# Gate and up with weights stationary, down one expert behind, and requests' rows on four column groups, in a two-layer decoder step

## The chip, the cores and the metric

One core of a Trainium2 chip. The time is that of one execution on the device, in microseconds. TensorE (PE) multiplies, VectorE (DVE) and ScalarE (ACT) work on the results, GpSimd (POOL) and SyncE (SP) mostly issue transfers. The stationary operand of a matmul is loaded into the array (PEld in the profile), the moving one streams past it. An f32 matmul appears as two records, each with its own weight load.

## What is computed

One inference step of two layers on 512 prompt rows and 8 rows of single-token requests, D = 1024, all in float32: an RWKV-7 time mix, then an attention over a shared K/V projection, and after each a mixture of 16 experts of which every row takes two.

```python
def hier_moe(x, w_gc, b_gc, w_gf, b_gf, w_gate, w_up, w_down):
    ...
    for e in range(MOE_EXPERTS):
        h = jax.nn.silu(xt @ w_gate[e]) * (xt @ w_up[e])
        y = y + comb[:, e:e + 1] * (h @ w_down[e])
    return y.reshape(shp)
...
    out = ((yn.astype(x.dtype) + bonus) * g) @ p['a_w_o'][l]
...
            kv_new = jnp.einsum('btd,dgsnh->btgsnh', x, p['b_w_kv'])
...
    return o.reshape(bq, t, B_HEADS_PER_GROUP * B_HEAD) @ w_o
```

`w_gate` and `w_up` are 1024 x 512 for each expert, `w_down` is 512 x 1024. The last three lines are the three row products: 520 rows by 1024 x 1024, 1024 x 1536 and 1024 x 1024.

## The kernel before

The stages run one after another, each in a block of its own that all engines leave together. Weights come in chunks of 1 MiB through a ring of slots: SP issues the load of a chunk when `slot_free` says that the chunk that held the slot is done with, PE waits for its landing in `take_chunk`. There are 6 slots, and 14 in an expert layer, which are filled while the stage before it still works.

`expert_layer` first finds each row's two experts and scatters the rows to DRAM, so that every expert has up to 96 rows in one place (`CAP`; rows beyond that go through a separate loop over spills, which the change leaves alone but for a tile that it shares). Then it loops over the 16 experts. POOL loads the 96 rows (`xe`), PE turns them in eight transposes (L1786), DVE copies them to `xT` (L1632). Gate and up (L1845) go by three sub-blocks of 32 tokens. The 32 tokens are the stationary operand and 256 columns of the weights move, 128 of gate and 128 of up; four column groups of the array hold the same tokens beside one another and each takes another 128 hidden columns. Over 8 pieces of k that is 32 matmuls a sub-block. ACT takes the sigmoid (L1734), DVE multiplies twice (L1637, L1639), PE turns the 128 x 128 hidden block (L1794), DVE copies it (L1643). Down (L1864) again has 32 tokens stationary in four column groups and 256 columns moving. ACT copies the results (L1740) and issues their stores (L1744). PE's order in an expert: gate and up, hidden turns 0 and 1, the next expert's turns of tokens, a drain that gives back a slot, hidden turn 2, down, a drain. An expert uses six chunks: four with two k each of gate and up, two of down.

The three row products are `output_rows` (L1341, called once in each layer) and the first part of `shared_kv` (L1934). They go by quarters or sixths of 256 output columns, one chunk each. For each, PE takes five tiles, four of 128 rows and one with the 8 request rows; the rows are stationary, 256 weight columns move, 8 pieces of k. DVE (L1353) or ACT (L1956) takes each tile out of PSUM. A drain gives back the slot.

## Time and profile before

| | us |
|---|---|
| median of 3 runs | 1977.13 |
| lowest, highest | 1972.67, 1979.21 |
| the profiled execution | 1974.3 |
| its span | 1972.5 |
| PE busy in it | 1609.8 |
| L1845, gate and up, busy | 194.4 + 155.6 |
| L1864, down, busy | 97.0 + 75.4 |
| L1934, busy | 108.1 |
| L1341, busy | 72.7 + 72.1 |

Busy times of a line are unions: matmuls in different column groups overlap and count once. The two figures of L1845 and L1864 belong to chunks in the two parts of the ring, those of L1341 to the two layers. Matmul records are about 0.2 us longer than the time after which the next one can follow, so rates are to be read from starts.

### The profile page before, as it was taken

How to read it: one execution, taken by the hardware profiler on the slowest of the kernel's cores; microseconds unless marked ns; L12 is line 12 of the kernel's file. 1: busy time of each engine (PE TensorE's matmuls, PEld its weight loads, DVE VectorE, ACT ScalarE, POOL GpSimd, SP SyncE). 2: the span in 40 equal slices, each digit the busy share in tenths (PEclk: the TensorE clock that was granted, in tenths of full speed). 3: DMA queues.
4: the chain of work that ended last, by engine and by line, in shares of the span. 5: the costliest groups of instructions: out<-in, count | busy, mean ns of one | idle time of the engine just before them, and what ended most of it. 6: DMA issues, size and time to landing. Idle time of an engine off the chain costs nothing. (4 is left out here: it accounts for less than half of the span.)

```text
span 1972.5 us, 46144 instructions
## 1 busy us (share of the span) xinstructions
PE 1609.8 (82%) x20428; PEld 1207.6 (61%) x20428; DVE 595.4 (30%) x1592; ACT 385.0 (20%) x929; POOL 234.1 (12%) x206
## 2 busy tenths in 40 slices
PE   7999999969942999997089899999995249999970
PEld 6778778856722666665067588888874126666650
DVE  5211646644143111111710200026613401111117
ACT  1123343315030011111201000125602100111112
POOL 1000135533022000000400000000001300000004
PEclk9999999988976999999589899999998679999995
DMA  9710001014217899994731344332011748999943
GB/s 311 305 50 1 0 22 36 26 40 147 78 64 282 313 384 390 387 383 140 270 41 43 118 110 99 98 74 88 25 64 64 270 155 315 383 387 383 378 153 139
DMA packets 221396, 345.98 MB, mean 175 GB/s; under 512 B 70056, under 2 KB 116944, under 8 KB 221200
## 3 DMA queue, kind: packets, MB, share of 16 engines
q1 hardware_dynamic: 193824, 289.38, 41.5%
q0 software_dynamic: 9856, 33.81, 5.6%
q10 hardware_dynamic: 17520, 19.84, 3.1%
q8 instruction: 164, 2.69, 0.6%
q14 instruction: 32, 0.26, 0.0%
HBM read 295.90 MB, written 47.11 MB: 174 GB/s over the span
## 5 line engine op out<-in xcount | busy, mean ns | idle before, releaser
L1845 PE MATMUL bank<-ring_extra,xT 128*32 128x256 f32 x3456 | 194.4, 380 | 9.2 <-issue 9.2
L2239 PE MATMUL bank<-x,ring 128*128 128x256 f32 (+1 forms) x768 | 174.5, 388 | 3.5 <-issue 2.7
L1845 PEld LDWEIGHTS bank<-ring_extra,xT 128*32 128x32 f32 x3456 | 133.9, 110 | 65.4 <-issue 17.3
L2239 PEld LDWEIGHTS bank<-x,ring 128*128 128x128 f32 x768 | 146.7, 193 | 28.0 <-issue 5.4
L1845 PE MATMUL bank<-ring,xT 128*32 128x256 f32 x2688 | 155.6, 386 | 7.3 <-issue 6.0
L1637 DVE TENSOR_TENSOR sg<-sg,bank 128x128 f32<-128x128 f32 x96 | 27.3, 285 | 377.8 <-ACT sg L1734 377.8
L1845 PEld LDWEIGHTS bank<-ring,xT 128*32 128x32 f32 x2688 | 102.1, 112 | 56.3 <-issue 15.1
L1934 PE MATMUL bank<-ring,x 128*128 128x256 f32 (+1 forms) x480 | 108.1, 386 | 2.5 <-PEq L2424 1.3
L395 PE MATMUL bank<-mix,ring 128*128 128x260 f32 x448 | 101.1, 385 | 0.7 <-issue 0.6
L1934 PEld LDWEIGHTS bank<-ring,x 128*128 128x128 f32 (+1 forms) x480 | 82.5, 174 | 28.2 <-issue 7.4
L1864 PE MATMUL bank<-ring_extra,hT 128*32 128x256 f32 x1728 | 97.0, 380 | 0.0
L395 PEld LDWEIGHTS bank<-mix,ring 128*128 128x128 f32 x448 | 84.4, 190 | 16.8 <-issue 3.2
L1734 ACT ACTIVATE sg<-bank 128x128 f32<-128x128 f32 x96 | 26.6, 277 | 341.8 <-PE bank L1845 341.8
L1864 PEld LDWEIGHTS bank<-ring_extra,hT 128*32 128x32 f32 x1728 | 55.7, 110 | 34.8
L1883 POOL DMA_DIRECT2D xe<-expert_in x32 | 16.3, 510 | 506.5 <-PE bank L1786 496.6
L1864 PE MATMUL bank<-ring,hT 128*32 128x256 f32 x1344 | 75.4, 380 | 0.0
L1740 ACT ACTIVATE yo<-bank 128x256 f32<-128x256 f32 x96 | 36.8, 383 | 193.0 <-PE bank L1864 193.0
L1341 PE MATMUL bank<-ring,w 128*128 128x256 f32 (+1 forms) x320 | 72.7, 389 | 1.8 <-PEq L1191 1.2
L1341 PE MATMUL bank<-ring,x 128*128 128x256 f32 (+1 forms) x320 | 72.1, 387 | 2.1 <-PEq L190 1.5
L1341 PEld LDWEIGHTS bank<-ring,w 128*128 128x128 f32 (+1 forms) x320 | 55.5, 175 | 19.3 <-issue 5.3
L1341 PEld LDWEIGHTS bank<-ring,x 128*128 128x128 f32 (+1 forms) x320 | 55.0, 174 | 18.9 <-issue 5.0
L1864 PEld LDWEIGHTS bank<-ring,hT 128*32 128x32 f32 x1344 | 43.4, 110 | 27.1
(374 smaller groups left out, 2324.7 us busy)
## 6 DMA issues: line engine op xcount, KB each, us to landing
ring_extra<-in_moe_w_gate SPq DMA_DIRECT2D x72, 512.0 KB, 9.6
ring_extra<-in_moe_w_up SPq DMA_DIRECT2D x72, 512.0 KB, 12.6
ring_extra<-in_moe_w_down SPq DMA_DIRECT2D x36, 1024.0 KB, 14.7
ring<-in_moe_w_gate SPq DMA_DIRECT2D x56, 512.0 KB, 9.4
ring<-in_moe_w_up SPq DMA_DIRECT2D x56, 512.0 KB, 12.1
ring<-in_moe_w_down SPq DMA_DIRECT2D x28, 1024.0 KB, 14.5
ring<-in_a_w_rkv SPq DMA_DIRECT2D x12, 1024.0 KB, 10.5
xe<-expert_in POOLq DMA_DIRECT2D x32, 384.0 KB, 7.7
```

Of the source, the lines that this page charges most:

```text
L395: ins = pe.matmul(pair(job, h)[:, 0:HALF], w[:, kt, q * 128:(q + 1) * 128], mix[n][:, kt, half(h)], start=kt == 0, stop=kt == KT - 1)
L1341: ins = pe.matmul(ps[job % 8][0:n, 0:256], z[:, kt, t * 128:t * 128 + n], w[:, kt, :], start=kt == 0, stop=kt == KT - 1)
L1637: dve.tensor_tensor(sg[:, u], sg[:, u], ps[i % 2][:, 0:128], ALU.mult).then_inc(gd, 1)
L1734: act.activation(sg[:, u], ps[i % 2][:, 0:128], ACT.Sigmoid).then_inc(sd, 1)
L1740: act.activation(yo[e % 2][:, u], ps[3 + i % 2][:, 0:256], ACT.Copy).then_inc(yc, 1)
L1845: ins = pe.matmul(ps[i % 2][32 * q:32 * q + 32, 0:256], xT[:, kt, 32 * u:32 * u + 32], gate_up(w[kt // 2], kt % 2, q), start=kt == 0, stop ...
L1864: ins = pe.matmul(ps[3 + i % 2][32 * r:32 * r + 32, 0:256], hT[:, u, 32 * k:32 * k + 32], w[k // 2].rearrange("p (k n) -> p k n", k=2)[:, ...
L1883: pool.dma_start(xe[e % 2][0:CAP, :], core.expert_in[CAP * e:CAP * e + CAP, :]).then_inc(xl[e % 2], 16)
L1934: ins = pe.matmul(ps[job % 6][0:n, 0:256], x[:, kt, t * 128:t * 128 + n], w[:, kt, :], start=kt == 0, stop=kt == KT - 1)
L2239: ins = pe.matmul(ps[2 * (job % 3) + h][:, 0:n], w[:, kt_, rr, :], z[:, kt_, lo:lo + n], start=kt_ == 0, stop=kt_ == 7)
```

## The change

Three things.

Gate and up: `weights_and_tokens` holds a 128 x 128 block of weights stationary and moves the 96 tokens of the expert past it. For each of 8 k, 4 blocks of hidden columns and the two matrices there is one matmul, into 96 columns of one of two PSUM banks (gate and up have a bank each, and two sets of banks alternate). The product comes out with the hidden columns on partitions, so nothing has to be turned before down; the turns of the hidden rows and their copies are gone. The sigmoid and the two multiplications work once an expert on 384 columns. Each of the first three chunks is given back right after its own matmuls, and the drains give way to an increment on the next product's first matmul.

Down, unchanged in shape, runs one expert behind: gate and up of e, turns of the tokens of e + 1, down of e - 1. The chunks are loaded in that order. Tokens and hidden values are in two tiles by turns; the second tile of tokens is `v_x` of the spills.

Requests' rows: the tile with 8 rows leaves the five-tile loop. `request_products` puts the 8 rows in four column groups, each with its own k, in two halves, so every group sums two of the eight pieces of k. DVE adds the four groups' results in four dependent operations on 8 rows. The other tiles rotate over six banks, the requests' over the last two. In `shared_kv` the same is done, with DVE for the requests' rows.

```diff
+def request_products(pe, bank, x, w):
+    for half in range(2):
+        for g in range(4):
+            kt = 4 * half + g
+            ins = pe.matmul(bank[32 * g:32 * g + REQ, 0:256], x[:, kt, SEQ:ROWS], w[:, kt, :], start=half == 0, stop=half == 1)
+    return ins
+
...
-                for t in range(TILES):
-                    if job >= 8:
-                        pe.wait_ge(ev, job - 7)
-                    n = tile_rows(t)
+                for t in range(4):
+                    if job >= 6:
+                        pe.wait_ge(ev, job - 5)
                     for kt in range(KT):
-                        ins = pe.matmul(ps[job % 8][0:n, 0:256], z[:, kt, t * 128:t * 128 + n], w[:, kt, :], start=kt == 0, stop=kt == KT - 1)
+                        ins = pe.matmul(ps[job % 6][:, 0:256], z[:, kt, t * 128:(t + 1) * 128], w[:, kt, :], start=kt == 0, stop=kt == KT - 1)
                     ins.then_inc(mm, 1)
                     job += 1
+                if q >= 2:
+                    pe.wait_ge(req_added, 4 * (q - 1))
+                request_products(pe, ps[6 + q % 2], z, w).then_inc(req, 1)
                 pe.drain().then_inc(core.slot_free, 1)
...
+            for q in range(4):
+                cols = slice(q * 256, (q + 1) * 256)
+                for t in range(4):
+                    job = 4 * q + t
+                    dve.wait_ge(mm, job + 1)
+                    r = rows[:, t, cols]
+                    dve.scalar_tensor_tensor(r, r, ALPHA, ps[job % 6][:, 0:256], ALU.mult, ALU.add).then_inc(ev, 1)
+                dve.wait_ge(req, q + 1)
+                r = rows[0:REQ, 4, cols]
+                dve.scalar_tensor_tensor(r, r, ALPHA, ps[6 + q % 2][0:REQ, 0:256], ALU.mult, ALU.add).then_inc(req_added, 1)
+                for g in range(1, 4):
+                    dve.wait_ge(req_added, 4 * q + g)
+                    dve.tensor_tensor(r, r, ps[6 + q % 2][32 * g:32 * g + REQ, 0:256], ALU.add).then_inc(req_added, 1)
...
-    for e in range(EXPERTS):
-        chunks += [((gate_view, up_view), (gate[e, :, 2 * j:2 * j + 2], up[e, :, 2 * j:2 * j + 2])) for j in range(4)]
-        chunks += [(lambda slot: slot.rearrange("p (k n) -> p k n", k=2), down[e, :, 2 * j:2 * j + 2]) for j in range(2)]
+    for e in range(EXPERTS + 1):
+        if e < EXPERTS:
+            chunks += [((gate_view, up_view), (gate[e, :, 2 * j:2 * j + 2], up[e, :, 2 * j:2 * j + 2])) for j in range(4)]
+        if e:
+            chunks += [(lambda slot: slot.rearrange("p (k n) -> p k n", k=2), down[e - 1, :, 2 * j:2 * j + 2]) for j in range(2)]
...
+        flat = lambda t: t[:, :, :].rearrange("p u k -> p (u k)")
...
+        x_e = [xT[:, :, :], v_x[:, 0:KT * CAP].rearrange("p (k t) -> p k t", k=KT)]
+        h_e = [flat(hT), flat(hid)]
+        gate_in, up_in = (0, 2), (1, 7)
...
+                def gated(e):
+                    dve.wait_ge(sd, e + 1)
+                    dve.tensor_tensor(flat(sg), flat(sg), ps[gate_in[e % 2]][:, 0:4 * CAP], ALU.mult).then_inc(gd, 1)
+                    dve.wait_ge(gd, e + 1)
+                    if e >= 2:
+                        dve.wait_ge(yd, SUBS * (e - 1))
+                    dve.tensor_tensor(h_e[e % 2], flat(sg), ps[up_in[e % 2]][:, 0:4 * CAP], ALU.mult).then_inc(hd, 1)
...
+                def sigmoid(e):
+                    act.wait_ge(gu, e + 1)
+                    if e:
+                        act.wait_ge(hd, e)
+                    act.activation(flat(sg), ps[gate_in[e % 2]][:, 0:4 * CAP], ACT.Sigmoid).then_inc(sd, 1)
...
+                def weights_and_tokens(e, freed):
+                    pe.wait_ge(xc, 2 * e + 2)
+                    if e >= 2:
+                        pe.wait_ge(hd, e - 1)
+                    for j in range(4):
+                        w = core.take_chunk(pe).rearrange("p (m k n) -> p m k n", m=2, k=2)
+                        for kt in (2 * j, 2 * j + 1):
+                            for ht in range(4):
+                                for m, bank in ((0, gate_in[e % 2]), (1, up_in[e % 2])):
+                                    ins = pe.matmul(ps[bank][:, CAP * ht:CAP * ht + CAP], w[:, m, kt % 2, 128 * ht:128 * ht + 128], x_e[e % 2][:, kt, :],
+                                                    start=kt == 0 and ht == 0, stop=kt == KT - 1 and ht == 3)
+                                    if freed:
+                                        ins.then_inc(core.slot_free, 1)
+                                        freed = False
+                        if j < 3:
+                            ins.then_inc(core.slot_free, 1)
+                    ins.then_inc(gu, 1)
+
+                def down(e, freed):
+                    pe.wait_ge(hd, e + 1)
+                    w = [core.take_chunk(pe).rearrange("p (k n) -> p k n", k=2) for _ in range(2)]
+                    for u in range(SUBS):
+                        i = SUBS * e + u
+                        if i >= 2:
+                            pe.wait_ge(yc, i - 1)
+                        for k in range(4):
+                            for r in range(4):
+                                at_k = CAP * k + 32 * u
+                                ins = pe.matmul(ps[3 + i % 2][32 * r:32 * r + 32, 0:256], h_e[e % 2][:, at_k:at_k + 32],
+                                                w[k // 2][:, k % 2, 256 * r:256 * r + 256], start=k == 0, stop=k == 3)
+                                if freed:
+                                    ins.then_inc(core.slot_free, 1)
+                                    freed = False
+                            if u == SUBS - 1 and k == 1:
+                                ins.then_inc(core.slot_free, 1)
+                        ins.then_inc(yd, 1)
...
-                for e in range(EXPERTS):
-                    pe.wait_ge(xc, 2 * e + 2)
-                    w = [core.take_chunk(pe) for _ in range(4)]
-                    for u in range(SUBS):
-                        i = SUBS * e + u
-                        if i >= 2:
-                            pe.wait_ge(hd, i - 1)
-                        for kt in range(KT):
-                            for q in range(4):
-                                ins = pe.matmul(ps[i % 2][32 * q:32 * q + 32, 0:256], xT[:, kt, 32 * u:32 * u + 32], gate_up(w[kt // 2], kt % 2, q),
-                                                start=kt == 0, stop=kt == KT - 1)
-                            if u == SUBS - 1 and kt in (1, 3, 5):
-                                ins.then_inc(core.slot_free, 1)
-                        ins.then_inc(gu, 1)
-                    turn_hidden(e, 0)
-                    turn_hidden(e, 1)
-                    if e + 1 < EXPERTS:
-                        turn_x(e + 1)
-                    pe.drain().then_inc(core.slot_free, 1)
-                    turn_hidden(e, 2)
-                    w = [core.take_chunk(pe) for _ in range(2)]
-                    for u in range(SUBS):
-                        i = SUBS * e + u
-                        pe.wait_ge(hc, i + 1)
-                        if i >= 2:
-                            pe.wait_ge(yc, i - 1)
-                        for k in range(4):
-                            for r in range(4):
-                                ins = pe.matmul(ps[3 + i % 2][32 * r:32 * r + 32, 0:256], hT[:, u, 32 * k:32 * k + 32],
-                                                w[k // 2].rearrange("p (k n) -> p k n", k=2)[:, k % 2, 256 * r:256 * r + 256], start=k == 0, stop=k == 3)
-                            if u == SUBS - 1 and k == 1:
-                                ins.then_inc(core.slot_free, 1)
-                        ins.then_inc(yd, 1)
-                    pe.drain().then_inc(core.slot_free, 1)
+                for e in range(EXPERTS + 1):
+                    if e < EXPERTS:
+                        weights_and_tokens(e, e >= 1)
+                        if e + 1 < EXPERTS:
+                            turn_x(e + 1)
+                    if e:
+                        down(e - 1, True)
+                pe.drain().then_inc(core.slot_free, 1)
```

## Rows read from the trace of the kernel before

**Rows 1.** The page: busy time by engine, then busy tenths in 40 slices; gate and up.
```profile
PE 1609.8 (82%) x20428; PEld 1207.6 (61%) x20428; DVE 595.4 (30%) x1592; ACT 385.0 (20%) x929; POOL 234.1 (12%) x206
...
PE   7999999969942999997089899999995249999970
...
L1845 PE MATMUL bank<-ring_extra,xT 128*32 128x256 f32 x3456 | 194.4, 380 | 9.2 <-issue 9.2
```

**Rows 2.** Timeline of one expert: start us, length us, engine, line, operation, count [idle before <-releaser].
```profile
760.64 1.01 DVE L1632 COPY xT<-bank 128x384 f32<-128x384 f32 x2
...
766.99 10.57 PE L1845 MATMUL bank<-ring,xT 128*32 128x256 f32 x192 [0.50 <-issue]
...
777.76 0.82 PE L1786 MATMUL bank<-const,xe 96*128 96x96 f32 x8
...
778.78 1.02 DVE L1632 COPY xT<-bank 128x384 f32<-128x384 f32 x2
...
779.01 0.30 PE L1794 MATMUL bank<-const,hid 128*128 128x128 f32 x1 [0.42 <-DVE hid L1639]
...
779.24 5.39 PE L1864 MATMUL bank<-ring,hT 128*32 128x256 f32 x96
```

**Rows 3.** Stretches: busy us (count) of five engines, PE clock, DMA share, GB/s.
```profile
654.00:891.00 237.00, 225.00 (x3915) 151.50 (x3911) 42.26 (x143) 26.14 (x79) 6.07 (x12) 1.00 1.04 385
891.00:903.00 12.00, 11.50 (x216) 7.88 (x212) 1.15 (x4) 1.32 (x4) 0.00 (x0) 1.00 0.88 332
...
1127.50:1130.50 3.00, 2.67 (x12) 2.63 (x12) 0.28 (x4) 0.00 (x0) 0.00 (x0) 0.50 0.94 307
1315.00:1328.00 13.00, 11.31 (x186) 9.31 (x184) 8.39 (x45) 8.19 (x24) 0.00 (x0) 1.00 0.25 82
```

**Rows 4.** Stretches of the first and second row product, columns as in the group before.
```profile
490.00:564.00 74.00, 72.69 (x320) 55.48 (x320) 8.38 (x20) 0.00 (x0) 0.00 (x0) 0.97 0.22 71
1001.80:1111.00 109.20, 108.00 (x480) 82.47 (x480) 0.00 (x0) 11.06 (x29) 2.00 (x3) 0.98 0.22 33
```

**Rows 5.** Timeline of a quarter of L1934: two full tiles, then eight rows.
```profile
1104.09 0.38 ACT L1956 ACTIVATE kv<-bank 128x256 f32<-128x256 f32 x1 [3.07 <-PE bank L1934]
...
1107.55 0.38 ACT L1956 ACTIVATE kv<-bank 128x256 f32<-128x256 f32 x1 [3.07 <-PE bank L1934]
1111.10 0.37 ACT L1956 ACTIVATE kv<-bank 8x256 f32<-8x256 f32 x1 [3.17 <-PE bank L1934]
```

**Rows 6.** Turns and weight loads by shape: busy us, mean ns of one | idle before.
```profile
L1786 PE MATMUL bank<-const,xe 96*128 96x96 f32 x256 | 27.8, 254 | 35.8 <-DMA xe<-expert_in 24.6 <-issue 11.2
...
L1864 PEld LDWEIGHTS bank<-ring_extra,hT 128*32 128x32 f32 x1728 | 55.7, 110 | 34.8
...
L1786 PEld LDWEIGHTS bank<-const,xe 96*128 96x128 f32 x256 | 24.9, 146 | 36.4 <-issue 36.4
...
L2186 PEld LDWEIGHTS bank<-kF,qF 64*128 64x128 f32 x256 | 21.5, 192 | 1.3
L2219 PEld LDWEIGHTS bank<-PT,v 128*64 128x64 f32 x448 | 18.4, 137 | 9.0 <-issue 5.9 <-ACT PT L2384 0.8
...
L1934 PEld LDWEIGHTS bank<-ring,x 128*8 128x8 f32 x96 | 8.2, 90 | 12.5 <-issue 2.0
```

**Rows 7.** Timeline of weight loads, at half and at full clock.
```profile
1128.21 0.54 PEld L2227 LDWEIGHTS bank<-att_const,relr 33*128 33x128 f32 x2
...
1128.64 0.54 PEld L2226 LDWEIGHTS bank<-att_const,relr 33*128 33x128 f32 x2
...
1129.92 0.54 PEld L2227 LDWEIGHTS bank<-att_const,relr 33*128 33x128 f32 x2
...
1323.13 0.53 PEld L2186 LDWEIGHTS bank<-kF,qF 64*128 64x128 f32 x8
```

**Rows 8.** Timeline: first load that waited for a slot; last result of the layer.
```profile
648.00 0.38 SPq L219 DMA_DIRECT2D ring<-in_moe_w_gate  x1
...
929.83 0.38 ACT L1740 ACTIVATE yo<-bank 128x256 f32<-128x256 f32 x1 [1.34 <-PE bank L1864]
```

More of the change, by code:

```diff
@@ L1347, in _ @@
         def _(dve):
-            for job in range(4 * TILES):
-                q, t = divmod(job, TILES)
-                n = tile_rows(t)
-                dve.wait_ge(mm, job + 1)
-                r = rows[0:n, t, q * 256:(q + 1) * 256]
-                dve.scalar_tensor_tensor(r, r, ALPHA, ps[job % 8][0:n, 0:256], ALU.mult, ALU.add).then_inc(ev, 1)
+            for q in range(4):
[11 more added lines that the diff above has]
+                    dve.tensor_tensor(r, r, ps[6 + q % 2][32 * g:32 * g + REQ, 0:256], ALU.add).then_inc(req_added, 1)
 def norm_rows(core, rows, layer, which, stores, combine=None, final_rows=None, then=None):
@@ L1744, in _ @@
                         act.dma_start(dst[r], yo[e % 2][32 * r:32 * r + 32, :, :]).then_inc(ys[e % 2], 16)
+                for e in range(EXPERTS + 1):
+                    if e < EXPERTS:
+                        sigmoid(e)
+                    if e:
+                        results(e - 1)
                 for b in range(2):
@@ L1928, in _ @@
                     w = as_k(256)(core.take_chunk(pe))
-                    for t in range(TILES):
+                    for t in range(4):
                         if job >= 6:
                             pe.wait_ge(ev, job - 5)
-                        n = tile_rows(t)
                         for kt in range(KT):
-                            ins = pe.matmul(ps[job % 6][0:n, 0:256], x[:, kt, t * 128:t * 128 + n], w[:, kt, :], start=kt == 0, stop=kt == KT - 1)
+                            ins = pe.matmul(ps[job % 6][:, 0:256], x[:, kt, t * 128:(t + 1) * 128], w[:, kt, :], start=kt == 0, stop=kt == KT - 1)
                         ins.then_inc(mm, 1)
                         job += 1
+                    if q >= 2:
+                        pe.wait_ge(req_added, 4 * (q - 1))
+                    request_products(pe, ps[6 + q % 2], x, w).then_inc(req, 1)
                     pe.drain().then_inc(core.slot_free, 1)
                 job = 0
+                pe.wait_ge(req_added, 24)
                 for g in range(3):
-                    pe.wait_ge(ev, 6 * TILES)
+                    pe.wait_ge(ev, 24)
                     for a in range(2):
@@ L1951, in _ @@
             def _(act):
-                for job in range(6 * TILES):
-                    q, t = divmod(job, TILES)
-                    n = tile_rows(t)
+                for job in range(24):
+                    q, t = divmod(job, 4)
                     act.wait_ge(mm, job + 1)
-                    act.activation(kv[0:n, t, q * 256:(q + 1) * 256], ps[job % 6][0:n, 0:256], ACT.Copy).then_inc(ev, 1)
-                act.wait_ge(ev, 6 * TILES)
+                    act.activation(kv[:, t, q * 256:(q + 1) * 256], ps[job % 6][:, 0:256], ACT.Copy).then_inc(ev, 1)
+                act.wait_ge(ev, 24)
+                act.wait_ge(req_added, 24)
                 for g in range(3):
@@ L1972, in _ @@
             def _(dve):
+                for q in range(6):
+                    dve.wait_ge(req, q + 1)
+                    r = kv[0:REQ, 4, q * 256:(q + 1) * 256]
+                    dve.tensor_copy(r, ps[6 + q % 2][0:REQ, 0:256]).then_inc(req_added, 1)
+                    for g in range(1, 4):
+                        dve.wait_ge(req_added, 4 * q + g)
+                        dve.tensor_tensor(r, r, ps[6 + q % 2][32 * g:32 * g + REQ, 0:256], ALU.add).then_inc(req_added, 1)
                 job = 0
```

38 lines of the change are left out of this document (10 added, 28 removed).

## The prediction

> **What bounds the kernel now.** I read the times and the totals first, then the slices, then the expert loop in order of time, then the DMA engines in the same stretch. The profiled execution took 1974.3 us for a span of 1972.5; the median shown is 1977.1, 2.8 above it. The sum below is made against 1974.3. TensorE (PE) is busy 82% of the span and no other engine over 30% [rows 1]; the slices show two long full stretches, the two expert layers [rows 1]. In one expert's turn [rows 2] the reader should see that PE has hardly a hole: gate and up start at 766.99, their 192 records (two for each f32 matmul, each with its own weight load) end 10.57 later, two turns of the hidden rows and, from 777.76, eight of the next tokens follow, then a hole of 0.42 before the third hidden turn, down from 779.24 for 5.39, and a hole of 0.50 ahead of gate and up, at the drain. The same point of two neighbouring experts (the first copy of x, 760.64 and 778.78) gives a period of **18.13 us**; 16 of them make 290 us of each layer.
>
> Close behind PE stand the transfers. From 654 to 891 us the DMA share is 1.04 at 385 GB/s [rows 3]: the DMA engines are full as well. One expert needs 6 MiB of weights, 0.39 MB of rows in and as much out, 7.08 MB, and 7.08 / 0.385 = 18.4 us. So PE's period of 18.13 and that of the transfers agree within 2%, and the ring's 14 slots, loaded ahead, cover the difference. This sets what each direction is worth: a slower PE costs in full, and a faster one gains only until the transfers are late.
>
> In the three row products (L1341 twice, L1934) PE is busy nearly all the time and the DMA share is 0.22 (two of the three are in [rows 4]); here PE alone bounds.
>
> **Gate and up, weights stationary.** Before: 3 sub-blocks of 32 tokens x 8 k x 4 column groups x 2 records = 192, four at a time, so 48 steps; the last record lasts 0.38 [rows 1], (10.57 - 0.38) / 47 = 0.217 us a step, 10.4 us in all [rows 2]. After: 8 k x 4 hidden blocks x 2 matrices = 64 matmuls, 128 records, none beside another, each with a load of 128 columns and 96 columns moving. A step of 256 moving columns takes 0.216 (tiles of 16 records are 0.38 + 3.07 = 3.45 apart [rows 5]), so 96 take 0.081, and 128 x 0.081 = 10.4 us: no gain and no loss if the loads are hidden. The question is the load. Its mean length by columns is 90 ns for 8, 110 for 32, 137 for 64, 192 for 128 [rows 6]; 192 - 137 over 64 columns is 0.86 ns a column, so 128 columns fill for about 0.11 us. At the half clock (0.50, [rows 3]) the rows of L2226 and L2227 show it bare: of five pairs of 128-column loads the first starts at 1128.21, the second at 1128.64 and the fifth at 1129.92, so 1.71 / 8 = 0.214 each, though 128, 32 or 1 columns move in between [rows 7]. Half of that is **0.107** at the full clock. At the full clock eight loads of L2186, two side by side, take 0.53: (0.53 - 0.19) / 3 = 0.113, with only 32 columns moving [rows 7]. So the loads bound this product, not the moving columns. I take 0.110 a record (0.107 plus the 3 ns by which a 256-column step exceeds 256 x 2 / 2.4): 128 x 0.110 = **14.1 us** against 10.4; ends 0.107 (13.7) and 0.117 (15.0: 0.113 with 0.004 for what such a row rounds).
>
> A row speaks for a lower price: the turns of L1786 have 128-column loads and 96 columns moving, and eight take 0.82, the last of them 0.25 [rows 6], so (0.82 - 0.25) / 7 = 0.081 each [rows 2]. But their load lasts 146 ns, not 192 [rows 6]; a turn's load is 56 ns over the 90 of an 8-column one, that of a product 102, so it fills in half the time. The Trainium skill (TensorE: Matmul & The Clock Gate, "LDWEIGHTS") puts a load at its columns over 1.2, about 107 ns for 128; the trace agrees, 0.107 from the half-clock rows. The Trainium skill's same page, "Back-to-back issue gap", says that a stream of load and matmul pairs at 128 columns keeps about 81 ns a matmul; by it gate and up would be 10.4 us, as in rival A below; no f32 product of the trace bears that out.
>
> **The rest of the expert's turn.** Removed: three turns of hidden rows with their copies, the hole before the third and the two drains. Left: eight turns of tokens 8 x 0.081 = 0.65, 0.15 extra when the array changes to column groups (last turn at 779.01 to first down at 779.24, 0.23 instead of 0.08), down 5.39 - 0.38 = 5.0 to its last step and about 0.31 from there to the next product (a step of 0.216 and 0.09 for the change of shape). New period: 14.1 + 0.65 + 0.15 + 5.3 = **20.2 us**, with ends 19.8 and 21.1. Against 18.13 that is +2.07 an expert, x 32 = **+66** (ends +53 and +95). The gate and up of an expert, done before the down of the previous one, hide the sigmoid and the two products on 384 columns (an estimate of 0.55 each, from the 384-column copies at 0.51 [rows 2]) under 5.3 us of down; if that cover failed PE would wait about 1.7 an expert. New waits: down waits for hd, which came a whole gate-and-up earlier; the vector engine's take waits for gu two experts back; the scalar engine's sigmoid queues before the three results of the previous expert, which wait for down anyway. I cost them at nothing. Once a layer expert 1's gate and up wait for the copy of its tokens with no down to cover it: 1.2 x 2 = +2.4. The tokens' loads on POOL's queue wait, as before, for the turns two experts back.
>
> Of the loads, each slot of gate and up is given back after its own quarter (some 3.5 us into the product) and not after the third sub-block, so the transfers start near 642 and not at 648 [rows 8]. At 20.2 us an expert they need 7.08 / 20.2 = 350 GB/s, below the 385 that they reach, so PE doesn't wait for them. Nothing of the layer's ends changes: last down, copy, store.
>
> **Requests' rows on four column groups.** Before, a quarter of a row product ends with 8 k x 2 records = 16 steps with 8 columns stationary; the copy of that tile comes 0.38 + 3.17 = 3.55 after the one before it, as long as a full tile [rows 5]. After: 2 halves x 2 records = 4 steps of four matmuls side by side, as L1845 runs now. Saved: 12 x 0.216 = 2.59 us a quarter; the change of shape (0.09) is there before and after. Quarters: 4 + 4 for L1341, 6 for L1934, 14: **-36.3 us**. All of it is on PE's path by [rows 4]. Added: three dependent additions on 8 rows after the last quarter of each stage, some 0.37 with the hand-over each by the 8-row copy of [rows 5], 1.1 x 3 = +3.3; elsewhere they lie beside the next quarter's 14 us. The vector engine's queue behind them holds only the next tile's addition, 3.4 us away. Six banks in place of eight: a bank is asked for six tiles (20 us) later. Net **-33 us** (ends -30 and -36).
>
> **Sum.** 66 + 2.4 - 33 = +35.4; 1974.3 + 35.4 = 2009.7, say **2010 us**. With the ends: 1974.3 + 53 + 2.4 - 36 = 1994 and 1974.3 + 95 + 2.4 - 30 = 2042.
>
> **Rivals.** *A, the loads hide and the transfers become the bound (faster).* If a record takes 0.081, the period on PE is 10.4 + 6.1 = 16.5, under the 18.4 of the transfers. These now run from 648 [rows 8] to about 902 (share 0.88 until 903 [rows 3]); begun 6 us earlier they end near 896, the last down needs 5.4 and its copy 0.4: 902, against 929.8 + 0.4 now [rows 8], -28 a layer. Less a few us for uneven landings: -25 x 2 - 33: about **1891 us**. It decides from a record below 0.100: there the period is 19.1 and the two parts cancel. For it: the turns at 0.081; against it: [rows 7]. *B, the requests' groups don't run side by side* (8 columns and different k in each): the 36 come back, **2046 us**. L1845 does just that with 32 columns, so little speaks for it. *C, load and moving columns add up:* 0.107 + 0.081 = 0.188 a record, 24 us, +10 more an expert, **2330 us**. Against it: a tile of L1934, 128 x 128 stationary and 256 columns moving, steps by 0.216 though a load of 0.107 belongs to each step [rows 5, 7]. The Trainium skill (TensorE: Matmul & The Clock Gate, "The mechanism") says that loads overlap matmuls only in another row group; by that it would be C, and those rows disagree. *D, the clock is at its lower level in the expert loop:* 128 x 0.214 = 27 us for gate and up, over 2300. Against it: 1315 to 1328, full of loads and turns, is granted 1.00 [rows 3].
>
> **How the numbers follow.** The forecast case 0.80, A 0.12, B 0.03, C 0.01, D 0.02, others 0.02. The forecast case alone spans 1994 to 2042. With B and a little on each side for uneven chunk landings the range is 1985 to 2052, and it leaves out A, C and D. Under 0.3% (6 us) a measurement of this kernel can't tell from no change: within that 0.02, faster 0.12, slower 0.86.
>
> **What would show it.** In the profile after: 128 gate-and-up records an expert, 0.110 apart, PEld nearly unbroken there; an expert period of 20.2; the DMA share below 1.0 in the loop; eight-row products of L1341 and L1934 in 0.9 us, quarters 15.3 apart and not 17.9. Wrong if the records stand 0.081 to 0.100 apart, if PE waits for landings, or if the groups of eight columns follow one another.

## The result and the profile after

The changed kernel took **2019.57 us** (2016.68 to 2021.99) against 1975.77 us (1972.67 to 1979.21) of the kernel before beside it: a ratio of 1.0221 (95% interval 1.0198 to 1.0244), 2.2% slower. The forecast was 2010 us, 1985 to 2052. The profiled execution took 2018.88 us for a span of 2017.1, 44.6 more than the 1974.3 of the one before. Its page, the lines that answer to [rows 1] (and the DMA line of the slices):

```profile
PE 1679.8 (83%) x18284; PEld 1405.5 (70%) x18284; DVE 576.8 (29%) x1416; ACT 371.8 (18%) x859; POOL 234.4 (12%) x206
...
PE   7999999969915999999079899999992379999980
...
DMA  9710010032156999993731344412114859999923
...
L1822 PE MATMUL bank<-spill_x,ring_extra 128*128 128x96 f32 x1152 | 131.2, 276 | 0.0
```

PE has 2144 records fewer and is busy 70 us longer. The timeline of one expert, as [rows 2] for before (start us, length us, engine, line, operation, count [idle before]):

```profile
750.52 14.37 PEld L1822 LDWEIGHTS bank<-xT,ring_extra 128*128 128x128 f32 x128 [0.41 <-issue]
750.52 14.53 PE L1822 MATMUL bank<-xT,ring_extra 128*128 128x96 f32 x128
...
764.89 0.82 PE L1810 MATMUL bank<-const,xe 96*128 96x96 f32 x8
765.09 0.49 ACT L1750 ACTIVATE sg<-bank 128x384 f32<-128x384 f32 x1 [14.05 <-PE bank L1822]
...
765.65 5.39 PE L1841 MATMUL bank<-ring_extra,hid 128*32 128x256 f32 x96
...
766.43 0.55 DVE L1660 TENSOR_TENSOR sg<-sg,bank 128x384 f32<-128x384 f32 x1
767.01 0.55 DVE L1664 TENSOR_TENSOR hT<-sg,bank 128x384 f32<-128x384 f32 x1
...
770.96 7.27 PE L1822 MATMUL bank<-spill_x,ring_extra 128*128 128x96 f32 x63
```

Read it so: gate and up are 128 records, the last of them 0.276 long, so (14.53 - 0.276) / 127 = 0.112 us each, and the row of their loads has no hole in 14.37 us. Then 0.76 for the turns, 5.31 for down, and from 750.52 to 770.96 the period is **20.44 us** against 18.13. Sigmoid and products lie under down. The stretches that answer to [rows 3] (busy us and count of PE, PEld, DVE, ACT and POOL, granted clock, DMA share, GB/s):

```profile
654.00:891.00 237.00, 237.00 (x2692) 209.31 (x2694) 24.45 (x48) 18.91 (x46) 6.06 (x12) 1.00 0.97 344
```

PE now has no hole, and the DMA engines have left their limit (0.97 at 344 GB/s for 1.04 at 385). The requests' rows, which answer to [rows 5]: in the first product two quarters and the additions behind the last, then two quarters of the product of L1962:

```profile
538.60 14.05 PE L1349 MATMUL bank<-ring,w 128*128 128x256 f32 x64 [0.29 <-issue]
552.58 1.05 PE L1325 MATMUL bank<-ring,w 128*8 128x256 f32 x16
...
553.70 0.41 DVE L1368 SCALAR_TENSOR_TENSOR rows<-rows,bank 8x256 f32<-8x256 f32 x1 [0.59 <-PE bank L1325]
...
554.14 1.32 DVE L1371 TENSOR_TENSOR rows<-rows,bank 8x256 f32<-8x256 f32 x3
...
1095.18 1.05 PE L1325 MATMUL bank<-ring,x 128*8 128x256 f32 x16
...
1110.50 1.05 PE L1325 MATMUL bank<-ring,x 128*8 128x256 f32 x16
```

Sixteen records in 1.05 us, and a quarter every 1110.50 - 1095.18 = 15.32 us where it was 17.87 (545.90 - 528.03, the starts of two quarters of L1341). The books of the two profiled executions: the expert loops, from the first gate and up to the last down, took 291.3 and 291.7 us and take 330.7 and 329.9, **+77.6**; the three stages of row products are 8.4, 9.0 and 13.3 shorter, **-30.7**; all the rest -2.3; sum +44.6.

### The profile page after: what moved, and what is told of

Read it like the earlier page. It is cut to its first block and busy times, and to the rows that moved or that the text cites. A ratio compares the mean times of both kernels' runs of the same rounds, so it can differ in the third digit from the quotient of the medians.

```text
span 2017.1 us, 41420 instructions
## 1 busy us (share of the span) xinstructions
PE 1679.8 (83%) x18284; PEld 1405.5 (70%) x18284; DVE 576.8 (29%) x1416; ACT 371.8 (18%) x859; POOL 234.4 (12%) x206
## 5 line engine op out<-in xcount | busy, mean ns | idle before, releaser
L1822 PEld LDWEIGHTS bank<-spill_x,ring_extra 128*128 128x128 f32 x1152 | 129.6, 192 | 3.3 <-issue 3.3
L1822 PE MATMUL bank<-spill_x,ring_extra 128*128 128x96 f32 x1152 | 131.2, 276 | 0.0
L1822 PEld LDWEIGHTS bank<-xT,ring 128*128 128x128 f32 x1024 | 120.7, 200 | 4.4 <-issue 2.5
L1822 PE MATMUL bank<-xT,ring 128*128 128x96 f32 x1024 | 122.2, 283 | 1.3 <-DVE xT L1656 1.3
L1822 PEld LDWEIGHTS bank<-xT,ring_extra 128*128 128x128 f32 x1024 | 115.1, 192 | 3.3 <-issue 3.3
L1822 PE MATMUL bank<-xT,ring_extra 128*128 128x96 f32 x1024 | 116.6, 276 | 0.0
L1822 PEld LDWEIGHTS bank<-spill_x,ring 128*128 128x128 f32 x896 | 100.8, 192 | 4.4 <-issue 2.5
L1822 PE MATMUL bank<-spill_x,ring 128*128 128x96 f32 x896 | 102.3, 276 | 1.6 <-DVE spill_x L1656 1.6
L1656 DVE COPY spill_x<-bank 128x384 f32<-128x384 f32 x32 | 16.4, 553 | 292.7 <-PE bank L1810 292.7
L1962 PE MATMUL bank<-ring,x 128*128 128x256 f32 x384 | 87.2, 389 | 2.6 <-PEq L2463 1.3
L1962 PEld LDWEIGHTS bank<-ring,x 128*128 128x128 f32 x384 | 74.5, 195 | 16.0 <-issue 5.6
L1349 PE MATMUL bank<-ring,x 128*128 128x256 f32 x256 | 57.9, 388 | 2.2 <-PEq L190 1.5
```

Source lines behind the costliest of these rows:

```text
L1349: ins = pe.matmul(ps[job % 6][:, 0:256], z[:, kt, t * 128:(t + 1) * 128], w[:, kt, :], start=kt == 0, stop=kt == KT - 1)
L1656: dve.tensor_copy(x_e[e % 2][:, 4 * h:4 * h + 4, :], ps[5 + h][:, :].rearrange("p (q t) -> p q t", q=4)[:, :, 0:CAP]).then_inc(xc, 1)
L1822: ins = pe.matmul(ps[bank][:, CAP * ht:CAP * ht + CAP], w[:, m, kt % 2, 128 * ht:128 * ht + 128], x_e[e % 2][:, kt, :], start=kt == 0 and ...
L1962: ins = pe.matmul(ps[job % 6][:, 0:256], x[:, kt, t * 128:(t + 1) * 128], w[:, kt, :], start=kt == 0, stop=kt == KT - 1)
```

## The experiments

The kernel before took 1975.87 us (median of 7) beside *rows_only*, *experts_only*, *groups2* and *groups4*, 1974.73 (median of 7) beside *move32*, *groups2_noload*, *groups4_noload* and *lag_only*, and 1973.63 (one run) beside the others. Where a kernel has no lowest and highest time below, it ran once, and what it decides is read from the periods and records of its trace. *move32*, *move64* and the four *noload* kernels leave out a part of the computation, as said with each.

**1. The parts alone.** *rows_only* has the requests' rows on column groups and the experts as before, *experts_only* the reverse:

```diff
 rows_only, against the kernel before
-                        ins = pe.matmul(ps[job % 8][0:n, 0:256], z[:, kt, t * 128:t * 128 + n], w[:, kt, :], start=kt == 0, stop=kt == KT - 1)
+                        ins = pe.matmul(ps[job % 6][:, 0:256], z[:, kt, t * 128:(t + 1) * 128], w[:, kt, :], start=kt == 0, stop=kt == KT - 1)
...
+                request_products(pe, ps[6 + q % 2], z, w).then_inc(req, 1)
 experts_only, against the changed kernel: the same lines the other way
```

> The expert layer as before, the requests' rows of the three row products on four column groups. Theory (the parts stand on PE's path one after another and add): the three stages were shorter by 8.4, 9.0 and 13.3 us in the changed kernel, so about 31 us under the kernel before, 1945 us. Rival (what the row products save is lost again, since the loads ahead for the expert layer then start from the same transfers and land late): less than half of it, 1960 us or more.

> The changed expert layer, the row products as before. Theory (parts add): 39.4 and 38.2 us more in the two expert loops, 2.8 less elsewhere, so 75 us over the kernel before, 2050 us. Rival (part of the loss of the changed kernel comes from the two changes meeting, for instance in the ring): 2035 us or less.

Both came out as their theories had it (1945 and 2050). Measured: rows_only 1942.97 us (1940.56 to 1951.48), ratio 0.9828 (0.9812 to 0.9845), -32.9. experts_only 2054.27 us (2049.85 to 2057.86), ratio 1.0393 (1.037 to 1.0415), +78.4, with periods of 20.44. -32.9 + 78.4 = +45.5 beside the measured +43.8: the parts add, and the slowdown is the experts' alone. What within the expert layer makes it, the order or the shape of gate and up, is split in experiment 6.

**2. What a record waits for: its load, the moving columns, or the transfers.** *move64* and *move32* let 64 and 32 of the 96 tokens move and leave out the hidden values of the others (here *move64*):

```diff
-                                    ins = pe.matmul(ps[bank][:, CAP * ht:CAP * ht + CAP], w[:, m, kt % 2, 128 * ht:128 * ht + 128], x_e[e % 2][:, kt, :],
+                                    ins = pe.matmul(ps[bank][:, CAP * ht:CAP * ht + 64], w[:, m, kt % 2, 128 * ht:128 * ht + 128], x_e[e % 2][:, kt, 0:64],
```

*after_noload* is the changed kernel whose weight loads end with the third expert (the down weights' line is changed the same way); PE then computes with what lies in the slots:

```diff
-            chunks += [((gate_view, up_view), (gate[e, :, 2 * j:2 * j + 2], up[e, :, 2 * j:2 * j + 2])) for j in range(4)]
+            chunks += [((gate_view, up_view), (gate[e, :, 2 * j:2 * j + 2], up[e, :, 2 * j:2 * j + 2]) if e < 3 else None) for j in range(4)]
```

> The changed kernel, but only the first 32 of the 96 tokens move past each block of weights in gate and up; the hidden values of the others are left out. The loads stay as they are. Theory (a record is bound by its load of 128 columns): records stay 0.107 to 0.112 us apart, the expert's period stays at 20.1 to 20.44 us, the time within 10 us of the changed kernel's 2020. Rival (the moving columns bound, at a price above 2 per clock): records come near a third of 0.112, at least under 0.08, and the period falls under 17 us.

> The changed kernel with 64 of the 96 tokens of an expert moving in gate and up; the other 32 tokens' hidden rows aren't computed. Theory (a record lasts as long as its load of 128 columns, whatever moves): where the granted clock is 1.00 the record stays at 0.112 us and the period at 20.4; if the clock holds at 1.00 in the expert loop the time is 2020. Rival (part of the record is its moving columns, 96 of them 0.081): the record falls towards 0.10 and the period towards 19. A run with 32 columns moving fell to the lower clock in the loop; if this one does too, its records there last 0.214 and the time is between 2150 and 2400.

> The changed kernel without the weight loads of the experts from the third on (they compute with what the slots hold). Theory: at a period of 20.44 us nothing waits for a transfer and the loads of 128 columns bound the product, so the period stays at 20.4 and the whole time within 6 us of the changed kernel's 2020. Rival (weights or instruction transfers take part in the 20.44 by delays too small to be seen as waits): the record falls from 0.112 to 0.107 or less, the period to 19.8, the time to about 2000.

Timelines of PE: move64 at the start of the loop and one expert later on, then move32; then two stretches of move64, three of move32, and one of after_noload:

```profile
624.75 27.57 PE L1822 MATMUL bank<-xT,ring 128*128 128x64 f32 x128 [0.65 <-DVE xT L1656]
...
689.44 14.51 PE L1822 MATMUL bank<-xT,ring_extra 128*128 128x64 f32 x128
...
704.54 5.39 PE L1841 MATMUL bank<-ring,hid 128*32 128x256 f32 x96
709.86 14.51 PE L1822 MATMUL bank<-spill_x,ring 128*128 128x64 f32 x128
```

```profile
692.78 24.83 PE L1822 MATMUL bank<-xT,ring_extra 128*128 128x32 f32 x128
```

```profile
670.00:685.00 15.00, 15.00 (x84) 13.79 (x87) 2.13 (x4) 0.49 (x1) 0.51 (x1) 0.50 0.41 138
685.00:700.00 15.00, 15.00 (x175) 12.80 (x167) 0.00 (x0) 1.16 (x3) 0.00 (x0) 0.99 0.90 305
```

```profile
758.50:763.00 4.50, 4.50 (x43) 4.50 (x42) 0.00 (x0) 0.06 (x1) 0.00 (x0) 1.00 0.91 259
765.00:780.00 15.00, 15.00 (x72) 15.00 (x73) 0.00 (x0) 0.00 (x0) 0.00 (x0) 0.50 0.69 253
700.00:1000.00 300.00, 300.00 (x2141) 266.73 (x2141) 19.17 (x36) 14.80 (x36) 4.57 (x9) 0.61 0.64 222
```

```profile
700.00:900.00 200.00, 200.00 (x2283) 175.85 (x2283) 20.37 (x40) 16.46 (x40) 5.07 (x10) 1.00 0.16 41
```

With a third of the moving columns gone a record at the full clock still takes (14.51 - 0.27) / 127 = 0.112 us, and the period is 20.42. With two thirds gone it does too: in the whole trace of move32 the starts of gate-and-up records lie 0.112 us apart wherever the granted clock was 1.00 (median of 1005), and 0.213 apart at 0.50 (median of 3059; move64 the same). So move32 has answered its question, though not by its period. With the weights' transfers gone (DMA share 0.16 for 0.97) the period is 20.44 in every expert and the time 2018.7 us. So neither the moving columns nor the transfers are in the 0.112: what is left is the load of 128 columns, or a price for each record, which experiment 3 tells apart.

The expected period and time came out for after_noload. For move32 both missed: 2401.1 us, since the mean granted clock was 0.61 in its expert loop. move64 had the half clock until about 683 us, 58 us into its loop, and 1.00 from there on (the second loop, 355.3 long, is like the first, 355.6), and took 2069.7 us, neither the 2020 of a full clock nor the 2150 to 2400 of a half one. In move32 the clock went to and fro: it rose to 1.00 during down (256 columns moving) and fell to 0.50 again within the first 6 us of the next gate and up; the rows 758.50 and 765.00 lie on both sides of such a fall. Why these two kernels were granted less is not settled by these runs.

**3. Take the load off: column groups.** If a load of 128 columns costs 0.107 because it is filled column by column, two loads of 64 columns in two column groups should go side by side. If instead each record has a price of its own, the pair takes longer than one record did, not less. *groups2* does that with every gate and up product, *groups4* with four groups of 32:

```diff
-                                    ins = pe.matmul(ps[bank][:, CAP * ht:CAP * ht + CAP], w[:, m, kt % 2, 128 * ht:128 * ht + 128], x_e[e % 2][:, kt, :],
-                                                    start=kt == 0 and ht == 0, stop=kt == KT - 1 and ht == 3)
+                                    for c in range(0, 128, 64):
+                                        ins = pe.matmul(ps[bank][c:c + 64, CAP * ht:CAP * ht + CAP], w[:, m, kt % 2, 128 * ht + c:128 * ht + c + 64], x_e[e % 2][:, kt, :],
+                                                        start=kt == 0 and ht == 0, stop=kt == KT - 1 and ht == 3)
```

> The changed kernel, but each 128-column block of weights is split into two blocks of 64 columns in two column groups, with the same 96 tokens moving past both. Same numbers are computed. Theory (a record of gate and up is bound by filling 128 columns, and column groups fill side by side, as a pair of L2219 suggests): two records take 0.081 us, 96 moving columns, gate and up 10.4 us and not 14.4, PE's period 16.5 us; then the transfers bound at about 18.4 us an expert and the time is 1890 to 1905 us, with PE waiting for landings. Rival (the 0.112 us are a price per moved block or per instruction, not of the load's columns): two records take 0.112 or more and the time is 2015 us or more. Second rival (loads of column groups fill one after another): no gain, 2015 to 2030 us.

> As the run with two groups, but four blocks of 32 columns in four column groups. Theory: four records in 0.081 us if PE can start eight instructions in that time; the transfers bound, so the same 1890 to 1905 us. Rival (issue binds: in the kernel before, four records with their loads start some 7 ns apart within a step of 0.216 us, which leaves open how fast they can go on): four records take over 0.11 us and the time is no better than that of the changed kernel, 2010 us or more.

Timeline of groups2 and a line of its DMA queues, then the timeline of groups4:

```profile
743.19 3.19 PE L1823 MATMUL bank<-xT,ring_extra 128*64 128x96 f32 x71 [0.71 <-issue]
746.31 0.88 PE L1810 MATMUL bank<-const,xe 96*128 96x96 f32 x8
747.12 5.39 PE L1842 MATMUL bank<-ring_extra,hid 128*32 128x256 f32 x96
752.44 5.80 PE L1823 MATMUL bank<-spill_x,ring_extra 128*64 128x96 f32 x128
758.07 3.47 PE L1823 MATMUL bank<-spill_x,ring 128*64 128x96 f32 x80
762.25 2.20 PE L1823 MATMUL bank<-spill_x,ring 128*64 128x96 f32 x48 [0.71 <-issue]
...
q8 instruction: 25, 0.41, 1.1%
```

```profile
745.67 2.84 PE L1823 MATMUL bank<-spill_x,ring 128*32 128x96 f32 x128 [0.93 <-issue]
752.71 7.13 PE L1823 MATMUL bank<-spill_x,ring 128*32 128x96 f32 x256 [4.19 <-issue]
```

groups2 took 1935.64 us (1930.6 to 1937.55), ratio 0.9788 (0.9768 to 0.9808). The record went as expected: the pair stands (3.47 - 0.25) / 39.5 = 0.082 us from the next (the 80 records of 758.07, a single one being 0.25 long), as 96 moving columns want. A price for each record is excluded by it, and what halving the load takes away was the load's.

The time didn't: 1890 to 1905, with waits for landings, was expected, and PE waited for no landing. PE now stands still ahead of 743.19 and 762.25 with nothing to wait for but "issue", and the periods are 18.28 and 18.00 on average in the two layers (from the third token turns on), not 16.5. Between those two holes lie 71 + 8 + 96 + 128 + 80 = 383 records, three times 128 within one record. The q8 line is the trace's queue of instructions from 700 to 860 us, 25 packets of 16 KB. All 31 such holes of over 0.3 us in the two loops have the same marks: they lie a whole multiple of 128 records apart, within the three records that the trace may lack, and the first record behind one starts 1.3 to 1.6 us after such a packet has landed, while the last chunk of weights had landed anything from 0.1 to 3.0 us before.

groups4 has 616 records an expert and took 2153.51 us (2149.07 to 2159.4), ratio 1.089 (1.0867 to 1.0913), with holes of up to 4.5 us behind 128 records or a multiple, 87 and 89 us of them in the two loops, and again each 1.2 to 1.6 us behind a packet. Its mean granted clock from 655 to 860 us was 0.92, so a part of its loss is the lower clock. Between holes its four records go in (2.84 - 0.25) / 31 = 0.084 us: that half of its theory held and the rival's over 0.11 didn't, though the rival's time did (2010 or more). So PE was short of instructions, and two causes stood against each other: their packets queue behind the weights, or they come at a limited rate anyway.

**4. The same without weights on the DMA engines.** *groups2_noload* and *groups4_noload* are these two with the edit of after_noload.

> The run with two column groups of 64, but the weights of experts from the fourth on are not loaded (PE reads what lies in the slots). In the run with loads PE stood still for 0.6 to 1.7 us once or twice an expert, each time until about 1.4 us after a transfer of instructions had ended, and never until a landing of weights. Theory (PE outruns its instruction stream because that stream's transfers queue behind those of the weights): without the weights the holes are gone and the period is 16.5 us, so a time near 1900 us. Rival (fetching instructions has a rate of its own): holes of the same length stay and the period stays at 18 us.

> The run with four column groups of 32 without the weights of experts from the fourth on. With loads PE worked through 128 records in 2.84 us and then stood for up to 4.7 us; the period was 24.6 us for 616 records, 5.1 us for 128. Theory (the weights' transfers hold the instructions up): the period falls to 16.5 to 18 us. Rival (a rate of its own, of one transfer of 128 records' instructions in some 5 us): the period stays above 23 us.

Timeline of groups2_noload, then of groups4_noload:

```profile
743.27 5.45 PE L1823 MATMUL bank<-spill_x,ring 128*64 128x96 f32 x128
...
749.47 5.39 PE L1842 MATMUL bank<-ring,hT 128*32 128x256 f32 x96
754.78 5.50 PE L1823 MATMUL bank<-xT,ring 128*64 128x96 f32 x128
```

```profile
768.04 2.85 PE L1823 MATMUL bank<-spill_x,ring 128*32 128x96 f32 x128 [0.62 <-issue]
771.78 1.20 PE L1823 MATMUL bank<-spill_x,ring 128*32 128x96 f32 x48 [0.90 <-issue]
```

groups2_noload has lost its holes: period 16.84 throughout (16.5 expected), 1895.2 us. So at this density of records the queueing behind the weights makes them. groups4_noload has kept short ones of 0.3 to 1.2 us, still 1.2 to 1.6 us behind a packet though no weights land any more, and the period is 19.13 and 19.47 on average where 16.5 to 18 or above 23 was expected; 1981.6 us. Neither cause alone is right for it: of the 25.1 and 25.9 us of groups4, 6.0 and 6.4 go with the weights (the clock is back at 1.00 with them), and 2.3 to 2.6 us over the 16.84 of groups2_noload stay with 616 records an expert.

**5. What the delay of one expert is worth.** *no_lag* puts down right behind its own gate and up (PE's part; the order of the chunks and ScalarE's loop follow it):

```diff
-                for e in range(EXPERTS + 1):
-                    if e < EXPERTS:
-                        weights_and_tokens(e, e >= 1)
-                        if e + 1 < EXPERTS:
-                            turn_x(e + 1)
-                    if e:
-                        down(e - 1, True)
+                for e in range(EXPERTS):
+                    weights_and_tokens(e, e >= 1)
+                    if e + 1 < EXPERTS:
+                        turn_x(e + 1)
+                    down(e, True)
```

> The changed kernel with down of an expert right behind its own gate and up and the next expert's token turns, not one expert behind. The computation is whole. Theory: the delay of one expert is what hides the sigmoid (0.49 us in the changed kernel's trace) and the two products (0.54 and 0.55) with their hand-overs; without it PE does the eight token turns (0.7 us) and then waits about 1.2 to 2.0 us an expert: period 20.44 + 1.2..2.0 = 21.6 to 22.4 us, 32 x that over the changed kernel's 2020, less one last down (5) a layer that no longer hangs behind: 2050 to 2075 us. Rival (down could stand right behind at no price, because the sub-blocks' products were hidden before as well): period 20.4 and 2020 us. A second rival: the wait also idles the array enough that the granted clock falls; then the clock in the loop is below 1.00 and the time over 2200.

Two experts in its timeline and the stretch of the first down:

```profile
746.14 6.88 PE L1839 MATMUL bank<-ring,hT 128*32 128x256 f32 x96 [1.90 <-DVE hT L1664]
752.95 14.53 PE L1820 MATMUL bank<-spill_x,ring 128*128 128x96 f32 x128
767.31 0.83 PE L1808 MATMUL bank<-const,xe 96*128 96x96 f32 x8
770.04 5.39 PE L1839 MATMUL bank<-ring_extra,hid 128*32 128x256 f32 x96 [1.90 <-DVE hid L1664]
775.36 14.53 PE L1820 MATMUL bank<-xT,ring_extra 128*128 128x96 f32 x128
```

```profile
746.10:752.90 6.80, 6.76 (x96) 3.35 (x96) 0.00 (x0) 0.77 (x2) 0.00 (x0) 0.77 0.61 205
```

2126.7 us, above the 2050 to 2075 of the theory and below the 2200 of the second rival. The wait is 1.90 us, and where nothing else happens the period is 775.36 - 752.95 = 22.41, +1.97: so far the theory. But in 25 of 28 the period is 23.9 to 24.1: behind the wait down takes 6.88 to 7.08 and not 5.39, at a mean clock of 0.77. The second rival was half right: the clock does fall, for a part of down only. The two together are 3.5 us in most experts.

**6. The order alone.** *lag_only* keeps the tokens stationary as before, but takes over the order: down one expert behind, no drains, the three hidden turns and their copy in one behind down, and the requests' rows of the change. *lag_noload* is that without the weights' transfers from the fourth expert on.

```diff
 lag_only, against the changed kernel
-                                    ins = pe.matmul(ps[bank][:, CAP * ht:CAP * ht + CAP], w[:, m, kt % 2, 128 * ht:128 * ht + 128], x_e[e % 2][:, kt, :],
+                                ins = pe.matmul(ps[i % 2][32 * q:32 * q + 32, 0:256], xT[:, kt, 32 * u:32 * u + 32], gate_up(w[kt // 2], kt % 2, q),
...
+                    if e < EXPERTS:
+                        turn_hidden(e)
```

> The requests' rows as in the change and down one expert behind, but gate and up as in the kernel before (32 tokens stationary, 256 columns moving, four column groups), with the three hidden blocks turned together after the previous expert's down. Theory (the stationary weights are what costs, the lag by itself is a gain, since it hides the hole before the third turn and the drains): PE's period 10.3 + 0.65 + 0.15 + 5.3 + 0.6 for the hidden turns = 17.0 us against 18.13, and with the requests' rows about 1910 us; if the transfers cannot follow below some 17.9 us an expert, 1930 us. Rival (the lag costs as much as it hides, or the transfers bound at 18.1 already): no better than the run with the requests' rows alone, 1943 us.

> The kernel with only the order changed (tokens stationary as before, down one expert behind, the three hidden turns together; requests' rows on four column groups) without the weight loads of the experts from the third on (they compute with what the slots hold). Theory: its late periods of 19 to 21 us come from weights that arrive late, PE's own period is 17.1 us: all periods are 17.1 and the loops about 274 us each and not 280, the time 1905 to 1910 against 1919.6. Rival (the late periods come from PE or from instruction transfers of their own): they stay, and the time is 1919.

Timeline of lag_only, first an expert in the middle, then a late one; its waits on landings from 650 to 900 us; its stretch; and a stretch of lag_noload:

```profile
739.96 0.88 PE L1814 MATMUL bank<-const,xe 96*128 96x96 f32 x8
...
740.78 5.39 PE L1851 MATMUL bank<-ring_extra,hT 128*32 128x256 f32 x96
...
746.09 0.55 PE L1838 MATMUL bank<-const,hid 128*128 128x128 f32 x3
...
757.07 0.88 PE L1814 MATMUL bank<-const,xe 96*128 96x96 f32 x8
```

```profile
831.61 0.55 PE L1838 MATMUL bank<-const,hid 128*128 128x128 f32 x3
833.99 12.25 PE L1826 MATMUL bank<-ring,xT 128*32 128x256 f32 x192 [1.83 <-DMA ring<-in_moe_w_up]
```

```profile
PE bank L1826 <- DMA ring<-in_moe_w_up: 2.0, 2, 1.8
```

```profile
655.00:860.00 205.00, 203.17 (x3528) 121.87 (x3530) 37.93 (x106) 23.34 (x71) 6.09 (x12) 0.99 1.04 384
```

```profile
700.00:900.00 200.00, 200.00 (x3506) 118.97 (x3508) 37.57 (x106) 23.02 (x70) 4.55 (x9) 1.00 0.18 44
```

lag_only took **1919.55 us** (1914.17 to 1920.58), ratio 0.9714 (0.9687 to 0.9741): faster than both kernels, and between the 1910 and the 1930 that were expected. The period is 757.07 - 739.96 = 17.11, as expected (17.0), for ten experts of a layer; then the weights come late, 833.99 is the first case, and the late periods of the two layers are 20.69, 17.38, 19.05 and 19.43. Not all of that is waiting: behind the wait of 1.83 us the product takes 12.25 and not 10.57, at a mean clock of 0.72 from 834 to 840 us. The DMA share is 1.04 at 384 GB/s, as in [rows 3]. Without the weights' transfers all periods are 17.10 and the loops 275.6 and 275.9 us for 279.8 and 280.8: the late periods were the transfers'. The time of lag_noload, 1918.2 us, doesn't show it, against 1905 to 1910 expected: its first gate and up starts at 635.2 us and not at 629.7, before any difference between the two. That start, behind the landing of the first tokens, lay between 623.1 and 635.2 us in kernels with the same work ahead of it. Why is open, and it is why loops are compared here and not single times.

This splits the change. The two expert loops took 292.7 + 292.1 = 584.7 us in rows_only, 279.8 + 280.8 = 560.6 in lag_only and 330.7 + 329.9 = 660.6 in the changed kernel, all three with the same requests' rows. So the new order, with its joined hidden turns and without drains, gives 24.1 us (23.4 by the times), and the stationary weights, with their turns of hidden rows saved, take 99.9 (100.0 by the times).

## Why the prediction was right

The forecast case came true, by its own steps, and the measured time is 10 us above the forecast. The profiled execution is 9.2 above the sum of 2009.7: the loops are 9.2 over and the requests' rows 2.3 over, and the -2.3 of all the rest, which the sum didn't have, cancels the latter by chance.

| step | forecast | measured |
| --- | --- | --- |
| gate and up record | 0.110 (0.107 to 0.117) | 0.112 |
| expert period | 20.2 (19.8 to 21.1) | 20.44 |
| both loops | +68.4 | +77.6 |
| requests' rows, net | -33 (-36 to -30) | -30.7; alone -32.9 |
| DMA share in the loop | below 1.0 | 0.97 |
| eight-row product; quarters | 0.9 us; 15.3 us apart | 1.05; 15.32 apart |

- **The record.** The price was read from loads at the half clock with 1 to 128 columns moving [rows 7], and not from the turns at 0.081 or from the columns that move. move64, move32 and after_noload show that this was the right row: 0.112 at the full clock with 96, 64 or 32 columns moving, with transfers and without. The Trainium skill (TensorE: Matmul & The Clock Gate, "LDWEIGHTS") has a load at its columns over 1.2, 107 ns here; the trace agrees within 5 ns, 112 from load to load at the full clock, and 213 at the half one. The Trainium skill's same page has a "Back-to-back issue gap" of about 81 ns a matmul; it is met by no product of 128 stationary columns here (two records a matmul, 112 ns each); what lies near it are the records of the token turns (81) and the pairs of 64 (82).
- **Mis-sized: the loops by 9 us.** The period is 0.24 longer than forecast, which is the record's 128 x 0.002, and 32 x 0.24 = 7.7 us; the periods give 32 x (20.44 - 18.13) = 73.9. The remaining 3.7 lie at the start (2.4 forecast): expert 1's wait for its copy was 0.8 us and not 1.2, but the first gate and up began at the half clock. It took 17.45 and 17.25 us in the two layers for 14.53 at the full clock, where before it was 12.06 and 12.51 for 10.57: 1.4 and 0.8 us more. 2 x 0.8 + 1.4 + 0.8 = 3.8. That the longer product has more of itself in the slow beginning was not in the sum.
- **Mis-sized: the additions.** On PE a quarter, or in L1962 a sixth, saves 17.87 - 15.32 = 2.55 (2.59 forecast), 35.7 in all. The profiled stages give back 5.0 of it and not 3.3, 1.7 a stage and not 1.1: the three additions take 1.32 and stand behind the 0.41 of the first.
- **The cover.** The delay of one expert was costed as hiding 1.7 us. It hides 1.97, and with it a fall of the clock that would have cost another 1.5 in most experts; the prediction had no term for that fall.
- **The transfers.** They were said to be no bound at 20.2 us and to be one from 18.4 downwards. The first is shown by after_noload. The second is near: lag_only goes at 17.1 with 384 GB/s for ten experts of each layer and then waits for landings, and lag_noload doesn't. That it is the ring's lead that has run out by then is argued, not measured.
- **Rivals.** A (loads hide) was wrong as to the record, but its way is open: groups2 shows the 0.082, for twice as many records, and then PE waits for instructions and not for landings, which no rival had. Its threshold was slightly off: at 0.100 a record the period is 12.8 + 6.1 = 18.9 and not 19.1, so gain and loss cancel between 0.101 and 0.102. B is excluded by 16 records in 1.05 us, C by 0.112 against 0.188: with 96 columns moving, 0.081 by themselves, a load of 0.107 costs 0.005 more than itself. D didn't happen with 96 columns; with 32 moving its mechanism did for most of the loop, at a mean clock of 0.61 and 2401 us.

## What to carry over

Before making the weights stationary, price a record as the larger of its load (0.107 us for 128 columns of f32 at the full clock, 0.112 in a row of them) and its moving columns (0.081 for 96). The load decided at 96, 64 and 32 moving columns and the moving columns at 256 (0.216); the two meet near 128, an estimate from 0.216 / 2 = 0.108. Two groups of 64 columns brought the pair back to 0.082. Read the order of the work and the shape of the product apart: here the new order was worth a gain of 24 us in the loops (1919.6 us with the old shape), and the new shape cost 100. Without the delay of one expert the changed kernel would have cost 107 us more (2126.7, one run). Shorter records want more instructions, and these come over the same DMA engines as the weights.

## What was not expected of the hardware

- PE can run out of instructions: with some 0.04 us a record and full DMA engines it stood 0.3 to 1.4 us every 128 to 640 records (groups2), and with 0.02 us a record up to 4.5 us (groups4); without the weights' transfers the first vanished and the second shrank to 0.3 to 1.2 us.
- PE was busy without a hole in three kernels that differ in their moving columns alone, and the granted clocks were not the same: 1.00 from about 635 us on in the changed kernel (96 columns), from about 683 us on in move64, and a mean of 0.61 from 700 to 1000 us in move32, in turns of 0.50 and 1.00. A single wait of 1.90 us ahead of down was followed by a mean clock of 0.77 in most experts, and by 1.00 in others (770.04 in no_lag).
